# Score products of two heads on the two row halves of TensorE, in an attention loop of two heads a step

## The reference, cut to what matters

```python
# first_block: layer 0 (NSA and differential attention), layer 1 (MoBA), an MLP behind each
ls = jnp.einsum('bgrqd,bgqnkd->bgrqnk', qb, k_sel) * scale + bias_s      # "sel", 8 heads of 64
lw = jnp.einsum('bgrqd,bgkd->bgrqk', qb, kwb) * scale + ...              # "win", 8 heads of 64
logits = jnp.einsum('bmhqd,bmhkd->bmhqk', qb, k) * scale + ...           # "diff0", "diff1": 4 heads each
lo = jnp.einsum('bhqd,bhkd->bhqk', qb, k_own) * scale + ...              # layer 1: 16 heads of 64
p = masked_softmax(logits, mask);  o = p @ v
# second_block, layers 2 and 3
cols = split_columns(rms_norm_2(x, norm_g[layer]) @ w_in[layer])
y_gdn  = gdn_branch(cols, ...)     # gated delta net, 6 heads of 64, both directions
y_mla  = mla_branch(cols, ...)     # latent attention, 6 heads
y_rwkv = rwkv7_branch(cols, ...)   # RWKV-7, 4 heads of 64, both directions
x = x + (concatenate([y_gdn, y_mla, y_rwkv]) * silu(cols['gate'])) @ w_out[layer]
```

## Time and profile before

| | |
|---|---|
| median of 3 runs | 1379.41 us (1375.02 to 1384.25) |
| the profiled execution | 1374.13 us, span of its instructions 1372.3 us |
| its mean granted clock of TensorE | 0.965 |
| TensorE busy | 1286.6 us, 94% |
| VectorE busy | 745.9 us, 54% |
| ScalarE busy | 345.2 us, 25% |

### The profile page before, as it was taken

One profiled execution on the slowest core, in us unless ns is written; L12 is line 12 of the kernel. 1 busy time (PEld: TensorE's weight loads), 2 busy tenths in 40 slices (PEclk: granted clock), 3 DMA queues, 4 the chain that ended last, 5 costly groups with the idle time before them and its releaser, 6 DMA issues. The chain is left out here.

```text
span 1372.3 us, 17770 instructions
## 1 busy us (share of the span) xinstructions
PE 1286.6 (94%) x6965; PEld 932.9 (68%) x6965; DVE 745.9 (54%) x1425; ACT 345.2 (25%) x745; POOL 51.9 (4%) x92
## 2 busy tenths in 40 slices
PE   4989989999998999999999699999899899998997
PEld 4968647996446675599844387668577686575783
DVE  0245366666452123477743448965875269657672
ACT  2234321211001134112200322244341231334322
POOL 2000000000000000000000000200200000203000
PEclk9879999999999999999999899999999999999999
DMA  9711305444553331245544332220010541210000
GB/s 264 246 63 62 123 0 184 154 157 182 183 184 120 125 123 62 101 148 182 184 169 165 141 128 103 81 105 1 1 47 1 187 151 62 70 55 1 1 2 31
DMA packets 65978, 149.21 MB, mean 109 GB/s; under 512 B 2225, under 2 KB 8263, under 8 KB 65895
## 3 DMA queue, kind: packets, MB, share of 16 engines
q1 hardware_dynamic: 62608, 141.67, 29.5%
q0 software_dynamic: 1216, 3.52, 1.0%
q10 hardware_dynamic: 2071, 2.87, 0.7%
HBM read 146.96 MB, written 1.07 MB: 108 GB/s over the span
## 5 line engine op out<-in xcount | busy, mean ns | idle before, releaser
L432 PE MATMUL banks<-hnT,weight_slabs 128*128 128x256 f32 x672 | 154.9, 393 | 4.2 <-DVE hnT L1789 2.8
L1317 ACT ACTIVATE region<-banks 128x384 f32<-128x384 f32 (+8 forms) x154 | 74.4, 483 | 327.4 <-PE banks L432 138.2
L432 PEld LDWEIGHTS banks<-hnT,weight_slabs 128*128 128x128 f32 x672 | 132.0, 198 | 26.7 <-DVE hnT L1789 5.6
L482 PE MATMUL banks<-weight_slabs,region 128*128 128x512 f32 x256 | 115.1, 592 | 0.0
L1929 DVE TENSOR_TENSOR region<-banks,region 128x128 f32<-128x128 f32 x40 | 11.7, 292 | 153.6 <-PE banks L595 153.0
L482 PEld LDWEIGHTS banks<-weight_slabs,region 128*128 128x128 f32 x256 | 48.5, 190 | 60.3 <-issue 60.3
L482 PE MATMUL banks<-region 128*128 128x512 f32 x192 | 87.6, 592 | 0.0
L1772 DVE TENSOR_TENSOR region<-region 128x256 f32<-128x256 f32 (+23 forms) x160 | 75.7, 473 | 17.5 <-ACT region L1659 12.1
L1772 DVE TENSOR_TENSOR region<-weight_slabs 128x1024 f32<-128x1024 f32 x32 | 39.2, 1225 | 80.6 <-PE banks L482 76.4
L1772 DVE TENSOR_TENSOR region<-weight_slabs,region 128x1024 f32<-128x1024 f32 x64 | 78.2, 1222 | 1.1
L1273 POOL TENSOR_TENSOR region<-region,consts 128x240 f32<-128x240 f32 (+24 forms) x60 | 34.4, 599 | 1020.1 <-DVEq L1781 997.3
(11 more groups left out here) (353 smaller groups left out, 2073.1 us busy)
## 6 DMA issues: line engine op xcount, KB each, us to landing
weight_slabs<-in_mlp_w SPq DMA_DIRECT2D x32, 2048.0 KB, 8.6
weight_slabs<-in_w_in SPq DMA_DIRECT2D x10, 2048.0 KB, 7.7
weight_slabs<-in_od_w_in SPq DMA_DIRECT2D x6, 2048.0 KB, 8.1
weight_slabs<-in_ev_w_in SPq DMA_DIRECT2D x5, 2048.0 KB, 8.5
weight_slabs<-in_w_out SPq DMA_DIRECT2D x4, 2048.0 KB, 8.7
weight_slabs<-in_ev_w_out SPq DMA_DIRECT2D x2, 2048.0 KB, 8.3
weight_slabs<-in_od_w_out SPq DMA_DIRECT2D x2, 2048.0 KB, 7.9
weight_slabs<-in_w_in SPq DMA_DIRECT2D x2, 2016.0 KB, 7.6
```

Of the source, the lines that this page charges most:

```text
L432: ins = mm(view(ps, b + i * S, (1, S)), view(slabs, o + k * width + c0, (1, P)), view(hnT, k * S, (1, S)), start=k == 0, stop=k == KC - 1)
L482: ins = mm(view(ps, b, (1, 512)), view(R, act + k * st, (1, P)), view(w, wt + k * step_, (1, 512)), start=n == 0 and k == 0, stop=n == 7 a ...
L1317: say(A(dst, view(ps, b, *(dims or ((1, n),)), np_=np_), ACT.Copy, scale=scale), read("scalar", *key))
```

## The change

The loop of `attention` goes in steps of two heads. A step opens two banks and issues the 128-column products of both heads, then the 256-column products of both. It has the extras and fills of both, then the values of units i-4 and i-3, then the transposes of units i-2 and i-1. FILL, PIECE_AT and the places of the compressed attention are set anew. The chunk matrices of two heads, and the Gram products of two banks, are issued in turns between the halves, with the fills of both behind.

```diff
-FILL = ({**{i: 2 if i < 10 else 3 for i in range(14)}, 14: 4, 15: 4, 16: 4, 17: 4, 21: 3, 22: 3, 23: 2, 24: 2, 25: 2},
-        {**{i: 5 for i in range(6)}, 6: 2, 7: 4, 8: 4, 9: 4, 10: 4, 13: 3, 14: 3, 15: 2, 16: 2, 17: 2})
-PIECE_AT = ({3: 0, 7: 1, 11: 2, 13: 3, 15: 4, 17: 5}, {1: 0, 3: 1, 4: 2, 6: 3, 8: 4, 10: 5})
+FILL = ({**{i: 2 if i < 10 else 3 for i in range(14)}, 14: 3, 15: 3, 16: 3, 17: 3, 18: 2, 19: 2, 22: 3, 23: 3, 24: 3, 25: 3, 26: 2},
+        {**{i: 5 for i in range(6)}, 6: 2, 7: 4, 8: 4, 9: 4, 10: 4, 14: 4, 15: 4, 16: 4, 17: 2})
+PIECE_AT = ({3: 0, 7: 1, 11: 2, 13: 3, 17: 4, 19: 5}, {1: 0, 3: 1, 4: 2, 6: 3, 8: 4, 10: 5})
...
-                for i in range(N + 3):
+                def probs_T(u):
+                    key = ("PT", *units[u])
+                    pe.wait_ge(*at("probs_ready", *units[u]))
+                    b = open_(key, "unit")
+                    for j in range(3):
+                        ins = nc.tensor.transpose(view(ps, b + j * P, (1, P)), view(R, PB(u) + j * P, (1, P)), IDENT)
+                    close(ins, key)
+                def head_values(u):
...
+                for i in range(0, N + 4, 2):
                     if i < N:
-                        b = open_(("S", *units[i]), "unit")
-                        q, k = scores(*units[i])
-                        mm(view(ps, b, (1, P)), q(0, P), k(0, P), start=True, stop=True)
-                        close(mm(view(ps, b + P, (1, S)), q(P, P), k(0, S), start=True, stop=True), ("S", *units[i]))
+                        b = [open_(("S", *units[u]), "unit") for u in (i, i + 1)]
+                        qk = [scores(*units[u]) for u in (i, i + 1)]
+                        for hf, (q, k) in enumerate(qk):
+                            mm(view(ps, b[hf], (1, P)), q(0, P), k(0, P), start=True, stop=True)
+                        for hf, (q, k) in enumerate(qk):
+                            close(mm(view(ps, b[hf] + P, (1, S)), q(P, P), k(0, S), start=True, stop=True), ("S", *units[i + hf]))
                     extra(i)
+                    extra(i + 1)
                     if i == HALF_AT[L]:
                         mix_half(L, 0, "unit")
-                    if i == HALF_AT[L] + 1:
+                    if i == HALF_AT[L] + 2:
                         pe.wait_ge(*at("bank_read_by_scalar", "mixT", L, T - 1, 0))
                     fill(i)
...
+                    fill(i + 1)
+                    for u in (i - 4, i - 3):
+                        if u >= 0:
+                            head_values(u)
+                    for u in (i - 2, i - 1):
+                        if 0 <= u < N:
+                            probs_T(u)
...
-                if i in (3, 4):
-                    par = i - 3
+                if i in (4, 5):
+                    par = i - 4
...
-                if i in (9, 10):
-                    t = i - 9
+                if i in (10, 11):
+                    t = i - 10
...
-                    for s in range(8):
-                        c, h = divmod(s, 4)
-                        ct, hf = h // 2, h % 2
-                        b = open_(("M4", tag, s))
+                    for s in range(0, 8, 2):
+                        c, ct = s // 4, s % 4 // 2
+                        b = [open_(("M4", tag, s + hf)) for hf in range(2)]
                         for w in range(2):
...
-                        close(ins, ("M4", tag, s))
-                        fill(1)
+                            for hf in range(2):
...
+                                if w == 1:
+                                    close(ins, ("M4", tag, s + hf))
+                        fill(2)
...
                 for g in range(3):
-                    for i2 in range(2):
-                        b = open_(("G", L, g, i2))
-                        for i in range(2):
+                    b = [open_(("G", L, g, i2)) for i2 in range(2)]
+                    for i in range(2):
+                        for i2 in range(2):
```

More of the change, by code:

```diff
@@ new lines, in head_values @@
+                def head_values(u):
+                    name, h = units[u]
+                    vw = P if name[:4] == "diff" else HD
+                    per = 512 // vw
+                    if h % per == 0:
+                        ob[:] = [open_(("O", name, h // per, t), "long") for t in range(T)]
+                    pe.wait_ge(*at("bank_read_by_scalar", "PT", name, h))
+                    c = (h % per) * vw
+                    for j, t, k in ((0, 0, 0), (1, 1, 0), (2, 1, 1)):
+                        ins = mm(view(ps, ob[t] + c, (1, vw)), view(R, PTB(u) + j * P, (1, P)), values(name, h, k),
+                                 start=k == 0, stop=k == t)
+                        if k == t and h % per == per - 1:
+                            close(ins, ("O", name, h // per, t))
@@ L596, in attention @@
                     extra(i)
+                    extra(i + 1)
                     if i == HALF_AT[L]:
                         mix_half(L, 0, "unit")
-                    if i == HALF_AT[L] + 1:
+                    if i == HALF_AT[L] + 2:
                         pe.wait_ge(*at("bank_read_by_scalar", "mixT", L, T - 1, 0))
                     fill(i)
[L602 to L616, removed]
-                        pe.wait_ge(*at("bank_read_by_scalar", "PT", name, h))
-                        c = (h % per) * vw
-                        for j, t, k in ((0, 0, 0), (1, 1, 0), (2, 1, 1)):
-                            ins = mm(view(ps, ob[t] + c, (1, vw)), view(R, PTB(u) + j * P, (1, P)), values(name, h, k),
-                                     start=k == 0, stop=k == t)
-                            if k == t and h % per == per - 1:
-                                close(ins, ("O", name, h // per, t))
+                    fill(i + 1)
@@ L1054, in _ @@
                 for g in range(3):
-                    for i2 in range(2):
-                        b = open_(("G", L, g, i2))
-                        for i in range(2):
+                    b = [open_(("G", L, g, i2)) for i2 in range(2)]
+                    for i in range(2):
+                        for i2 in range(2):
                             c, h = divmod(4 * g + 2 * i + i2, 6)
                             m, hf = h // 2, h % 2
-                            ins = mm(view(ps, b + i * 256, (1, 256)),
+                            ins = mm(view(ps, b[i2] + i * 256, (1, 256)),
                                      view(R, GC + (3 + m) * S + c * P, (1, P), p0=64 * hf, np_=64),
                                      view(R, GC + m * S + c * P, (768, 2), (1, P), p0=64 * hf, np_=64), start=True, stop=True)
-                        close(ins, ("G", L, g, i2))
+                            if i == 1:
+                                close(ins, ("G", L, g, i2))
                 def mla_up(L=L):
```

7 lines of the change are left out of this document (4 added, 3 removed).

## The result

The changed kernel takes 1394.66 us in the median (1393.88 to 1398.33, 4 runs), the kernel before 1377.34 on the same chip (1375.02 to 1384.25). The ratio is 1.0123, interval 1.0079 to 1.0166: slower by 1.2%, where no change was forecast (1379 us, between 1361 and 1389). The profiled execution took 1395.32 us, its span is 1393.5 us.

The account below looks back on a forecast made before the run. TensorE was taken to bound both attentions, TensorE and VectorE nearly equally the RWKV stage. +3.2 us (first attention), -3.5 (second) and 0 (RWKV) summed to -0.3 us: 1379 us at the median, range 1361 to 1389.

Parts of the forecast that it names:

- The relief: On TensorE, score pairs on different halves overlap and share trips: 10.9 us saved in the first attention, 8.3 in the second.
- the sum: All gains and losses added: +3.2 us first attention, -3.5 second, 0 RWKV stage, giving -0.3 us.
- the moved compressed scores: In the first attention, moving the compressed scores was to cost at most 0.3 us either way.
- The waits at VectorE: In both attentions TensorE waits for VectorE: 0.56 us at several step entries, up to 3.1 us where heads are weighted.
- The clock: Half-speed spells behind TensorE pauses: 2.5 us in the first attention, 0.8 us more in the second.
- The pause in step 10: First attention: a new 3.1 us TensorE wait, with a clock cost of 1.7 to 3.4 us, taken as 2.5.
- Rival (b): New pauses in the attentions and before the inversions bring half-speed spells: 10 us slower, 1389 us; chance 0.15.
- (a): Attention waits don't bite because some cover keeps VectorE ahead: 20 us go, 1359 us; chance 0.22.
- (c): Row halves don't overlap in the score pairs, only trips are saved: 11.4 us less gain, 1390 us; chance 0.04.
- (d): Score pairs overlap but starts keep program order: 3.5 us less gain, 1382 us; chance 0.05.
- RWKV stage: Chunk matrices: VectorE's work bounds the stage, which ends 1.03 us earlier; set at 0 per layer, between -1.03 and +2.5.

Follow-up runs that it names:

- e3: The changed kernel with four buffers for the probabilities instead of three; 1377.16 us, ratio 1.0016 to the kernel before.
- e1: The changed attention loop alone, with chunk matrices and Gram products in the order of the kernel before; 1400.96 us, ratio 1.0141 to that kernel.
- e7: The changed kernel with a pair's score products issued head by head (128, 256, then 128, 256); 1401.14 us, ratio 1.0190 to the kernel before.
- e2: The kernel before's attention loop with the alternating chunk matrices and Gram products of the change; 1374.51 us, ratio 0.9954 to the kernel before.
- e5: The changed kernel with four probability buffers and the weighting of finished heads one head later; 1366.81 us, ratio 0.9931 to the kernel before.
- e12: The changed kernel with the weighting of finished heads one head later, three probability buffers kept; 1390.03 us, ratio 1.0096 to the kernel before.

## Why the prediction was wrong

**The relief: right in kind, set too large.** Work at full clock falls by 5.9 us in the second attention; the prediction's 8.3 less 1.7 for two more output products is 6.6 (the sum charged 0.2 for them, and the 1.5 come back behind the stage). In the first it falls by 5.2 to 5.6 where 9.9 less 1.7 were due. Most of what is missing is a step not in the prediction: I counted the moved compressed scores at "at most 0.3 us". In the kernel before they stand behind one head's scores on the other half and run at the same time:

```profile
88.60 0.37 PE L594 MATMUL banks<-region 64*128 64x128 f32 x1
88.61 0.39 PE L722 MATMUL banks<-region 64*128 64x15 f32 x2
...
89.19 1.37 PE L722 MATMUL banks<-region 64*128 64x15 f32 x11
90.50 1.99 PE L549 MATMUL banks<-hnT,weight_slabs 128*128 128x256 f32 x8
```

Scores and compressed scores take 1.9 us there, 3.8 for both steps. Behind a pair nothing is left to overlap with: 1.0 for the pair and, in e3 at full clock, 1.85 and 1.92 for the two, 4.8 us. With the old overlap, in which the compressed scores add 0.86 us to a head's, it would have been 1.0 + 2 x 0.86 = 2.8.

**The waits at VectorE: right in place and size.** 0.43 to 0.54 us at the entries (0.56 forecast), 0.80 and 0.81 at second transposes (0.98), 3.00 in step 10 (3.1), 2.95 at step 20 (2.7), 1.52 at step 12 of the second attention (1.4), 0.67 at step 22 (0.7). The idle time was too small by what I did not list: 1.20 and 2.16 us where the third bank of the half output projection waits for VectorE to read the residual, and ScalarE's copies, 0.82 us at the entry of step 10 and 1.14 behind the second attention's mix (where 0.2 was set). The first attention's idle time grew by 11.5 us (10.3 in the sum, less 0.4 for a wait that the moved products were to fill), the second's by 6.4 (3.8 in the sum, with the small ones).

**The clock: the step that failed.** "The pause in step 10 is new: 1.7 to 3.4 us, I take 2.5", and 0.8 for the second attention. The small waits had no price for the clock behind them. (The 2.6 us that it sets beside a row of 4.54 leave out the tail; by the eight records in 3.70 us six take 2.8.) The windows of the profile after, over three of the spells:

```profile
133.80:140.60 6.80, 6.24 (x20) 4.57 (x21) 2.60 (x10) 3.28 (x10) 0.00 (x0) 0.50 0.02 4
174.80:181.60 6.80, 6.80 (x29) 5.96 (x29) 1.86 (x7) 3.28 (x10) 0.00 (x0) 0.50 0.33 125
...
546.90:557.10 10.20, 9.08 (x33) 6.34 (x34) 2.81 (x10) 5.00 (x15) 0.00 (x0) 0.50 0.10 38
```

Half clock came behind three of the long waits and, as e3 shows, also where waits of 0.5 and 0.8 us stand close together. Its cost rose by 7.2 us in the first attention (1.9 in e1 and e7) and by 4.6 in the second: 11.8 (6.5) where the sum has 2.5 + 0.8, less 1.0 that the first pair was to save by running at half clock. Rival (b) had this mechanism at about its true size, 10 us, with the places partly wrong: it set 5 of the 10 us at the inversions, where in the profile after half clock cost 3.1 us behind that of layer 2 and 1.4 behind that of layer 3. I gave it 0.15, and had put it on top of a sum that was itself short in waits and relief.

In the terms of the sum, for the two attentions together: idle time 17.9 us where 13.7 were set, 4.2 more; half clock 11.8 where 2.3 were set, 9.5 more; relief at full clock 11.5 where 16.3 were set, 4.8 less. With the forecast -0.3 this makes the 18.2 us by which they are longer. The 2.5 ahead of the change, 1.3 and -3.0 behind the two attentions and 2.2 in layers 2 and 3 lead to the 21.2 of the spans. With the first attention of e1 and e7 in place of the one profiled here, the clock is 4.2 us more than set, and it is then no worse than the waits (4.2) and the relief (5.2): the clock is the largest miss, but only with the 5 us that may be one execution's.

**Rivals (a), (c), (d): out.** (a) fell with the waits. (c) and (d) fell with the rows at 504.90 (0.85 us for a pair; in the terms of the prediction it is 1.69 by (c) and 1.26 by (d)) and with e7. The Trainium skill, page TensorE: Matmul & The Clock Gate, Part 3, has matmuls start strictly in program order; for products on different row halves neither the profile after nor e7 agrees: in e7 the product that stands third starts 0.013 us after the first, ahead of the second.

**RWKV stage: right in the stage.** The inversion starts 1.0 us earlier (39.1 and 39.0 against 40.1 and 40.0 us), VectorE's busy time is untouched, TensorE idles 7 to 9 us, and the gain is given back behind it. From that inversion to the chunk matrices of layer 3 the profile after takes 3.2 us more than before, e2 1.1. Two rows of the profile after:

```profile
883.61 1.13 PE L962 MATMUL banks<-region 64*128 64x256 f32 x8 [2.71 <-DVE region L2410]
...
901.58 0.95 PE L796 MATMUL banks<-region,consts 128*128 128x240 f32 x2 [1.87 <-POOL region L1287]
```

## What to carry to other kernels

Work taken off the engine that bounds a stage is worth what its neighbours leave of it: when two heads are issued at once, each buffer and each bank is held for two heads, so give the buffers that one more place in the same edit (e3), and keep long work of the reading engine behind the read that the bound engine wants next (e5; without the fourth buffer, e12, this was worth only 2.8 us). A longer ring of banks was not tried. A pause of TensorE costs more than its length, since half clock may follow, so price small repeated waits by the clock behind them too. Compare stage by stage where an untouched stage can differ by 11 us from one execution to the next.

## What the runs showed of the hardware that was not expected

In the score pairs and the Gram products, products on different row halves are independent queues in effect: records of both start 0.007 to 0.043 us apart, in either order of issue. The same attention code took 123.4, 123.6 and 128.5 us in three kernels, with the same idle time, through spells of half clock alone. And a stage of 199.6 us took 210.6 with the same records at a mean clock of 0.90: what decides which of the two an execution gets was not found.
